# PEER expert retrieval: slots of 128 tokens and one expert each, against slots of 64 tokens and two

## The reference

```python
def blk(hb):                       # one block of 128 tokens
    q = (hb @ w_q).reshape(PEER_BLOCK, PEER_HEADS, 2, PEER_KEY_DIM // 2)
    sc = jnp.einsum('thpd,hpnd->thpn', q, sub_keys).astype(jnp.float32)
    s1, i1 = lax.top_k(sc[:, :, 0], PEER_TOPK)
    s2, i2 = lax.top_k(sc[:, :, 1], PEER_TOPK)
    cand = (s1[..., :, None] + s2[..., None, :]).reshape(PEER_BLOCK, PEER_HEADS, PEER_TOPK * PEER_TOPK)
    top_s, ci = lax.top_k(cand, PEER_TOPK)
    e = jnp.take_along_axis(i1, ci // PEER_TOPK, axis=-1) * N_KEYS \
        + jnp.take_along_axis(i2, ci % PEER_TOPK, axis=-1)
    gate = jax.nn.softmax(top_s, axis=-1).astype(hb.dtype)
    act = jax.nn.gelu(jnp.einsum('thkd,td->thk', u_tab[e], hb), approximate=False)
    return jnp.einsum('thk,thkd->td', gate * act, v_tab[e])
```

## Time and profile before

| | |
|---|---|
| median of 3 runs | 3402.43 us (3392.74 to 3404.69) |
| profiled execution | 3404.81 us, span 3403.0 us |
| PE | 2916.1 us busy, 86% |
| DVE | 2321.7 us, 68% |
| ACT | 1550.6 us, 46% |
| chain that ended last | PE 44%, DMA 27%, DVE 21% |
| moved by DMA | 1298.59 MB, mean 382 GB/s |
| of that, the gathers (queue q0) | 1140.92 MB, 82.3% of the 16 engines' time |

### The profile page before, as it was taken

How to read it: one execution, slowest core, us unless ns; L and a number is a source line. 1 busy time by engine, 2 the same in 40 slices (tenths; PEclk the granted TensorE clock), 3 DMA queues, 4 the chain that set the end, 5 groups by cost and what they waited for, 6 DMA issues and landing times.

```text
span 3403.0 us, 32496 instructions
## 1 busy us (share of the span) xinstructions
PE 2916.1 (86%) x9486; PEld 1498.2 (44%) x9486; DVE 2321.7 (68%) x5531; ACT 1550.6 (46%) x4211; POOL 1300.5 (38%) x1097
## 2 busy tenths in 40 slices
PE   7989899988889898989899878987898888787777
PEld 5755555543445444544444333533353344443222
DVE  1268738785687658774788578866876587677854
ACT  2147334554356344643456345644563455333333
POOL 0023324443344433343445434443444434343432
PEclk8998999999999999999999999999999999899899
DMA  4289999999999999999999999999999999799998
GB/s 173 90 318 362 385 384 405 392 406 418 417 392 388 422 422 408 392 399 417 421 396 414 422 421 422 405 421 422 400 373 418 422 353 330 299 373 421 372 422 346
DMA packets 238361, 1298.59 MB, mean 382 GB/s; under 512 B 45748, under 2 KB 70228, under 8 KB 95462
## 3 DMA queue, kind: packets, MB, share of 16 engines
q0 software_dynamic: 156672, 1140.92, 82.3%
q1 hardware_dynamic: 81510, 155.59, 12.2%
HBM read 1279.41 MB, written 16.44 MB: 381 GB/s over the span
## 4 chain that ended last, share of the span: by engine, by line
PE 44%; DMA 27%; DVE 21%; ACT 4%; issue 2%; POOL 0%; SPq 0%; DVEq 0%; ACTq 0%; POOLq 0%
PE PS L1080 21%; DMA R<-in_t_uv,idx 19%; DVE R L1728 8%; PE PS L763 8%; DMA R<-in_t_uv,idxS 4%; DMA wring<-in_w_out 2%; PE PS L844 2%; PE PS L1002 2%; PE PS L729 2%; PE PS L843 2%; DVE SC L1689 2%; DVE SC L1686 2%; DVE ef L1691 2%; DMA wring<-in_w_query 2%; PE PS L1029 2%
## 5 line engine op out<-in xcount | busy, mean ns | idle before, releaser
L1080 PE MATMUL PS<-R,diag 128*128 128x512 f32 x3616 | 1788.4, 630 | 295.8 <-ACT diag L1355 262.8
L694 POOL DMA_INDIRECT R<-in_t_uv,idx x1024 | 1236.6, 1208 | 1981.1 <-PE PS L1080 1236.6
L1728 DVE CUSTOM_DVE_ANT_0 R<-R,hb 128x1024 f32<-128x1024 f32 x1088 | 1316.3, 1219 | 663.0 <-DMA R<-in_t_uv,idx 581.8
L1080 PEld LDWEIGHTS PS<-R,diag 128*128 128x128 f32 x3616 | 672.1, 198 | 1172.3 <-issue 606.9
L1346 ACT ACTIVATE acts<-dots 128x1 f32<-128x1 f32 x1088 | 217.8, 200 | 1258.8 <-DVE dots L1728 1256.2
L1355 ACT ACTIVATE diag<-ident,wv 128x128 f32<-128x128 f32 x840 | 337.7, 402 | 46.3 <-PE PS L1080 19.3
L763 PE MATMUL PS<-R 128*128 128x256 f32 (+1 forms) x1280 | 296.1, 388 | 42.6 <-ACT stg L1123 36.4
L1348 ACT ACTIVATE wv<-gate,acts 128x1 f32<-128x1 f32 x1024 | 302.0, 295 | 33.2
L763 PEld LDWEIGHTS PS<-R 128*128 128x128 f32 x1280 | 245.9, 199 | 111.8 <-issue 80.2
L1739 DVE SCALAR_TENSOR_TENSOR xb<-R,wv,xb 128x1024 f32<-128x1024 f32 x184 | 235.7, 1281 | 9.5 <-ACT wv L1348 9.5
L1466 DVE CUSTOM_DVE_ANT_0 PP<-PS,mask 128x144 f32<-128x144 f32 (+7 forms) x64 | 49.4, 771 | 170.8 <-PE PS L844 170.7
(11 more groups left out here) (242 smaller groups left out, 2389.9 us busy)
## 6 DMA issues: line engine op xcount, KB each, us to landing
wring<-in_w_out SPq DMA_DIRECT2D x64, 512.0 KB, 12.0
wring<-in_w_query SPq DMA_DIRECT2D x64, 512.0 KB, 8.3
R<-in_t_win SPq DMA_DIRECT2D x27, 1024.0 KB, 12.0
R<-in_t_uv,idx POOLq DMA_INDIRECT x1024, 12.6
pr<-prd SPq DMA_DIRECT2D x8, 976.0 KB, 11.2
prd<-stg SPq DMA_DIRECT2D x54, 128.0 KB, 7.6
xb<-in_x_prompt SPq DMA_DIRECT2D x8, 512.0 KB, 8.5
R<-in_w_out SPq DMA_DIRECT2D x8, 512.0 KB, 4.7
```

The source lines that it names most:

```text
L694: e.indirect_dma_start(dst, None, table, bass.IndirectOffsetOnAxis(ap=index, axis=0)).then_inc(S[s], c.count(name, s, 16))
L1080: m = mm(bank(n), diag[:, NTH[s] % DR, :], pair(s)[:, D + 512 * n:D + 512 * n + 512], start=begins, stop=s == last_slot(t), skip_group_che ...
L1728: e.tensor_tensor_reduce(u, u, hb[:, tile_of(g) % 2, :], 1.0, 0.0, ALU.mult, ALU.add, dots[:, g % NW:g % NW + 1]).then_inc(dve_done, c.cou ...
```

## The change

A slot now holds 64 tokens and two experts of each. Partitions 0 to 63 hold the tokens with one expert, partitions 64 to 127 the same tokens with another. Slots of tokens 0 to 63 (half 0) and of tokens 64 to 127 (half 1) alternate; `place(r)` gives half and expert column of slot r: the first 8 slots of a tile are all of half 0, the last 8 of half 1, and in between they take turns. The number of slots and the bytes of each stay.

On PE `diag` becomes 128x64 (from `fold`, which has two identities of 64 on top of each other), so the product adds the two experts of each token and writes 64 partitions of PSUM, those of its half. There are 8 buffers of it. All 1024 prompt slots go to PE and none to DVE. The sample tile works as before, with two neighbouring buffers as one 128x128.

The input of a slot must stand on both halves of the partitions. So `hb` becomes `hn` (one tile's normed input) and `hh[half]`, filled by an ACT copy on the same partitions (`along`) and a DMA to the other 64 (`across`), 8 slots ahead of use. Indices and gates are written to `idxN` and `gateN`, and SP copies them to their places by four DMAs each per piece. To make room `wring` has two buffers, and `ef` shares `bposf`. The top search of the next tile begins 3 turns earlier and ends 4 turns earlier.

```diff
-DR = 4
+DR = 8
...
-def on_dve(s):
-    return s < P * NTILE and s % (4 if 4 <= s % P < 60 else 8) == 2
-
-
-BY_PE = [s for s in range(NSLOT) if not on_dve(s)]
-BY_DVE = [s for s in range(NSLOT) if on_dve(s)]
-NTH = {s: i for q in (BY_PE, BY_DVE) for i, s in enumerate(q)}
+def place(r):
+    quarter, k = divmod(r, 32)
+    if quarter in (1, 2):
+        half, n = k % 2, k // 2
+    elif k < 8:
+        half, n = 0, k
+    elif k < 24:
+        half, n = (k + 1) % 2, k // 2 - 4 + 8 * (k % 2)
+    else:
+        half, n = 1, k - 16
+    return half, 16 * quarter + n
...
-        spread(tail(t + 1), at + (52 if t > 1 else 58), at + 96)
-        spread(top(t + 1, 0), at + 96, at + 119)
+        spread(tail(t + 1), at + (52 if t > 1 else 58), at + 93)
+        spread(top(t + 1, 0), at + 93, at + 115)
...
-        wring = sb("wring", [P, 3, D])
+        wring = sb("wring", [P, 2, D])
...
-        idxS = sb("idxS", [P, NSMP], U32)
-        gateS = sb("gateS", [P, NSMP])
+        idxN = sb("idxN", [P, P], U32)
+        gateN = sb("gateN", [P, P])
...
-        hb = sb("hb", [P, 2, D])
-        diag = sb("diag", [P, DR, P])
+        hn = sb("hn", [P, D])
+        hh = sb("hh", [P, 2, D])
+        diag = sb("diag", [P, DR, 64])
...
-            return 4 if t == 1 else 3
+            return 4 if t == 1 else 2
...
-            return R[:, m % 4, :] if t == 1 else wring[:, m % 3, :]
+            return R[:, m % 4, :] if t == 1 else wring[:, m % 2, :]
...
-                if m == 2 and t > 2:
+                if m == 0 and t > 2:
...
                     yield from p.to(1 + m - nb - NCH)
                     load_w(t, m, p)
                 yield from p.to(8)
-                e.wait_ge(pe_done, c.at("pe", f"used q{t}_6"))
+                e.wait_ge(pe_done, c.at("pe", f"used q{t}_{NCH - 1}"))
                 dma(gfin, A["g_final"].partition_broadcast(P), "gfin", f"g{t}")
 
+            def norm2(p, t):
+                if t == 1:
+                    yield from p.to(3)
+                    e.wait_ge(pe_done, c.at("pe", "hT1"))
+                    across(0, 1)
+                    across(1, 1)
+
+            def across(half, t):
+                other = 1 - half
+                dma(hh[64 * other:64 * other + 64, half, :], hn[64 * half:64 * half + 64, :], f"hx{half}", f"h{t}")
+
+            def top(p, k):
+                t, piece = k // 4, k % 4
+                ne = P // pieces(t)
+                m = ne // 2
+                if t < SMP:
+                    for what, src, dst, sem in (("top", idxN, idx, "ix"), ("gate", gateN, gate, "gx")):
+                        yield from p.to(18 if what == "top" else 19)
+                        e.wait_ge(dve_done, c.at("dve", f"{what}{t}_{piece}"))
+                        for f in range(2):
+                            for half in range(2):
+                                at = 64 * half + m * piece
+                                dma(dst[64 * f:64 * f + 64, t % 2, at:at + m],
+                                    src[64 * half:64 * half + 64, ne * piece + m * f:ne * piece + m * f + m],
+                                    sem, f"{t}_{piece}" if f + half == 2 else None)
+
             def peer(g):
+                for t in range(2, NTILE + 1):
+                    if g == P * (t - 1) - 8:
+                        e.wait_ge(dve_done, c.at("dve", f"u{g - 1}"))
+                        across(0, t)
+                    if g == P * (t - 1):
+                        e.wait_ge(dve_done, c.at("dve", f"u{g - 1}"))
+                        across(1, t)
                 for t in range(1, SMP + 1):
                     if g == last_slot(t) + LAG + 3:
                         e.wait_ge(dve_done, c.at("dve", f"y{t}"))
...
-                    e.wait_ge(*spent(c, HOMES[s][1]))
+                    e.wait_ge(pe_done, c.at("pe", f"v{HOMES[s][1]}"))
...
-                    e.wait_ge(dve_done, c.at("dve", f"top{t}_{s % P * pieces(t) // P}"))
+                    e.wait_ge(S["ix"], c.at("ix", f"{t}_{s % P * pieces(t) // P}"))
...
-                    m = mm(bank(n), diag[:, NTH[s] % DR, :], pair(s)[:, D + 512 * n:D + 512 * n + 512],
-                           start=begins, stop=s == last_slot(t), skip_group_check=True)
+                    row = pair(s)[:, D + 512 * n:D + 512 * n + 512]
+                    if t == SMP:
+                        m = mm(bank(n), diagS[:, s % 4, :], row, start=begins, stop=s == last_slot(t), skip_group_check=True)
+                    else:
+                        m = mm(bank(n)[64 * half:64 * half + 64, :], diag[:, s % DR, :], row, start=s % P in (0, 8),
+                               stop=s % P in (119, 127), skip_group_check=True)
...
+            def moved(t):
+                for half in range(2):
+                    e.wait_ge(S[f"hx{half}"], c.at(f"hx{half}", f"h{t}"))
+
+            def along(half, t):
+                r = slice(64 * half, 64 * half + 64) if t < SMP else slice(0, P)
+                act(hh[r, half, :], hn[r, :], ACT.Copy).then_inc(act_done, c.count(f"hx{t}_{half}"))
+
...
-                    if h == 0 and t >= 3:
-                        e.wait_ge(dve_done, c.at("dve", f"u{last_slot(t - 2)}"))
-                    act(hb[:, t % 2, VD * h:VD * h + VD], bank(7, P, P + VD), ACT.Copy,
+                    if h == 0 and t > 1:
+                        moved(t - 1)
+                    act(hn[:, VD * h:VD * h + VD], bank(7, P, P + VD), ACT.Copy,
...
-                    act(wv[:, k:k + 1], gate_of(v), ACT.Copy, scale=acts[:, k:k + 1]).then_inc(act_done, c.count(f"w{v}"))
-                    if not on_dve(v):
-                        settle()
-                        n = NTH[v]
-                        if n >= DR:
-                            e.wait_ge(pe_done, c.at("pe", f"v{BY_PE[n - DR]}"))
-                        m = fold if tile_of(v) == SMP else ident
-                        act(diag[:, n % DR, :], m[:], ACT.Copy, scale=wv[:, k:k + 1]).then_inc(act_done, c.count(f"d{v}"))
+                    t = tile_of(v)
+                    if t < SMP and v % P % (P // pieces(t)) == 0:
+                        e.wait_ge(S["gx"], c.at("gx", f"{t}_{v % P * pieces(t) // P}"))
+                    act(wv[:, k:k + 1], gate_of(v), ACT.Copy, scale=acts[:, k:k + 1]).then_inc(act_done, c.count())
+                    settle()
+                    last = v - (4 if t == SMP else DR)
+                    if last >= 0:
+                        e.wait_ge(pe_done, c.at("pe", f"v{last}"))
+                    if t == SMP:
+                        dst, m = diagS[:, v % 4, :], fold[:]
+                    else:
+                        dst, m = diag[:, v % DR, :], fold[:, 0:64]
+                    act(dst, m, ACT.Copy, scale=wv[:, k:k + 1]).then_inc(act_done, c.count(f"d{v}"))
+                for t in range(2, SMP + 1):
+                    if g == P * (t - 1) - 8:
+                        e.wait_ge(dve_done, c.at("dve", f"u{g - 1}"))
+                        along(0, t)
+                    if g == P * (t - 1) and t < SMP:
+                        e.wait_ge(dve_done, c.at("dve", f"u{g - 1}"))
+                        along(1, t)
...
-                        act(hb[:, t % 2, :], xb[:, t % 2, :], ACT.Square, accum_out=peerv[:, 0:1]).then_inc(act_done, c.count())
+                        act(wring[:, 1, :], xb[:, t % 2, :], ACT.Square, accum_out=peerv[:, 0:1]).then_inc(act_done, c.count())
...
-                e.tensor_copy(idx[:, t % 2, cols], ef[:, hs, :].rearrange("p h k -> p (h k)")).then_inc(
+                e.tensor_copy(idxN[:, cols], ef[:, hs, :].rearrange("p h k -> p (h k)")).then_inc(
...
+                    t, half = tile_of(g), half_of(g)
+                    first = g - P * (t - 1) if g < P * NTILE + 8 else None
+                    if first == 0 or first == 8 and t < SMP:
+                        e.wait_ge(act_done, c.at("act", f"hx{t}_{half}"))
+                        if t < SMP:
+                            e.wait_ge(S[f"hx{half}"], c.at(f"hx{half}", f"h{t}"))
...
-                    e.tensor_tensor_reduce(u, u, hb[:, tile_of(g) % 2, :], 1.0, 0.0, ALU.mult, ALU.add,
+                    e.tensor_tensor_reduce(u, u, hh[:, half, :], 1.0, 0.0, ALU.mult, ALU.add,
...
-                v = g - LAG
-                if 0 <= v < NSLOT and on_dve(v):
-                    t, n = tile_of(v), NTH[v]
-                    e.wait_ge(act_done, c.at("act", f"w{v}"))
-                    if n and tile_of(BY_DVE[n - 1]) == t:
-                        e.wait_ge(dve_done, c.at("dve", f"x{BY_DVE[n - 1]}"))
-                    else:
-                        e.wait_ge(dve_done, c.at("dve", f"h{t}"))
-                    x = xb[:, t % 2, :]
-                    stt(x, pair(v)[:, D:2 * D], wv[:, v % NW:v % NW + 1], x, ALU.mult, ALU.add).then_inc(
-                        dve_done, c.count(f"x{v}"))
```

(25 more changed lines are left out.)

35 lines of the change are left out of this document (17 added, 18 removed).

## The result

| | before | changed |
|---|---|---|
| median | 3397.6 us (4 runs, 3386.7 to 3404.7) | 3523.5 us (4 runs, 3510.9 to 3526.4) |
| ratio | 1 | 1.0364, 95% interval 1.0339 to 1.0388 |
| profiled execution, span | 3404.8 us, 3403.0 us | 3522.0 us, 3520.2 us |

The changed kernel is slower by 3.6%, about 124 us. I forecast 3425 us and a range that ended at 3490.

What follows compares the result with a forecast made beforehand. The prediction took DMA's gathers, with a ceiling of 422 GB/s, to bound the kernel. Its terms -32 + 0 + 10 + 18 + 4 + 20 = +20 against 3404.8 us gave 3425 us, range 3365 to 3490.

Steps and rivals of the forecast that it cites:

- DVE's part: 184 rows of V leave DVE, 235.7 us of busy time mostly beside DMA; claimed to win 32 us.
- PE's products: PE gets 184 more V products; neighbours of opposite halves overlap in attention, waits for DMA hide the rest; cost 0.
- Rival (c): PE's column halves do not overlap, so attention's 14 extra products per tile cost +133; 3558 us, chance 0.12.
- Changes of the array's shape: Switching PE between 128-column and 64-column products, 0.1 to 0.2 us each, about three new per head; +10, bounds 0 and 29.
- New transfers: Copies of the normed input, indices and gates load the full DMA with bytes and packets; +18 us, bounds 0 and 25.
- the index's detour: SP must copy indices before POOL gathers; hidden at tile ends, exposed at the very start; +4 us (3 to 8).
- The weight ring: Matrix buffers for w_out and w_query go from three to two, so PE waits for loads; +20 us, range 0 to 112.
- rival (b): PE stands before each matrix and DMA runs dry in the tails; +60 us on top, 3465 us, chance 0.14.
- Rival (a): Relief wins: buffers come free in time and DMA is fed at 1.02 outside the sample stage; -37, 3368 us, chance 0.30.
- The DMA share in the long stretch: DMA's busy share from 600 to 2440 us, expected at 1.00 to 1.01; 1.02 near 411 GB/s would show relief winning.
- PE's waits for matrices: Sign in PE's waits for w_out and w_query loads: tens of us fit the forecast's own term, hundreds fit rival (b).
- The stretch from 2440 to 3040 us: Where the sample tile is attended; the forecast called itself wrong if this changed by more than 20 us.

## Why the prediction was wrong

The direction was right. So in the main was the bound: DMA's gathers set most of the pace, since 316 us more of work on PE cost 47. The size missed: 124 us in place of 20. By its own steps:

**DVE's part and PE's products (-32 and 0, together -32).** Measured +47 - 61 = -14. The sum is off by 18 us, and that it is no further off is luck, since the parts are not what I thought: PE's products with the relief cost 47, and it was turns that paid that back. What the relief alone is worth no run shows. Rival (c), halves that do not overlap, is dead by the rows with eight records in 1.94 us. The Trainium skill, "TensorE: Matmul & The Clock Gate", Part 3, says that matmuls in different column strips of 32 run at the same time. The trace agrees here for two halves of 64: two products take the time of one, a factor of 2.0.

**Changes of the array's shape (+10, bounds 0 and 29).** Measured +45, with what came along. "Three groups of V per head give about three new changes" is the step that failed. It was right for attention (some 200 changes) and left out the 400 to 500 of the other stages, above all the tails, where each matrix now costs two. The price of one stood in rows 5 and was right.

**New transfers (+18) and the index's detour (+4).** The copies with all seen loads ahead of them measured +28, near the sum. POOL waited for `idx` only at the very start, as forecast. The step that failed is the sentence on SP: "the waits for DVE's index stand before the weight loads of the next tile, which come 12 turns later, so nobody is late". It named only one of the things queued behind that wait. The load of `pr` stood right behind it (DVE waited 36.4 us; moving it won 15), and in tile 7 the cache loads stood between the wait and the weights (PE waited 27.4 us; moving them won 14 to 23). I had printed SP's order at a tile's end, where the first half's indices are, and not at turn 36, where the second half's are.

**The weight ring (+20, bounds 0 and 112).** The rival (b) asked for +60 more from it. (Its 3465 us is the kernel before plus 60; on top of the 20 already taken it would have been 3485.) Measured 21 in the kernel before and 36 in the changed one. Mechanism right, size within the bounds.

**Rival (a), relief wins (3368).** It did not come: even without copies and with the third buffer the kernel stays 0.9% above.

Of the signs that I named: the V products under 1871 us (that figure counts the sample tile's 256 records too; together they are 1606 + 128 = 1734), pairs within ns, DVE near 2090 (2106), the first gather 4 us later (5.0), and no rate over 422 GB/s all came. The DMA share in the long stretch was 0.99 and the rate 395 GB/s, below the 1.00 to 1.01 that I expected. PE's waits for matrices went to 154 us, between "tens" and "hundreds". The stretch from 2440 to 3040 us did change by more than 20 us: tile 7 alone took 47 more. That was the sign for "wrong", and it pointed at one of the places.

The range was too narrow since it went by the rivals, one at a time, and left no room for several terms that are off the same way. Shape (+35 over), SP's order (+29), the ring (+16), V (+18) and the copies (+6) all came out above what I took, 104 us together.

## What to carry to other kernels

When a wait is put on a queue that serves others, list everything behind it until the wait can end, at each place where it stands and not at one; here small copies of 1.05 MB in all cost 22 us themselves and some 29 more by what stood behind SP's wait for them. When a new shape of matmul comes in, count its neighbours in the whole program: here the price was paid per change, some 600 times, and it was won back only where two halves ran at once. A buffer that is free for part of a tile (the score buffer between two searches) can be worth more than the change that was planned: as a fourth weight buffer it made the kernel before 0.3% faster.

## What the hardware showed beside

Two products of 64 columns on opposite halves of the array, float32, 512 columns moving, take 1.94 us together and one takes 1.93. A wait of PE for a matrix costs more than itself: in the changed kernel's longest wait, 27.4 us in which PE stood, the granted clock falls from 0.96 to a mean of 0.57, near the lower of its two levels (1.2 of 2.4 GHz), and the matrix behind it takes 3.65 us where others take 1.98. The windows there (columns as before):

```profile
2640.00:2680.00 40.00, 31.69 (x146) 14.46 (x142) 27.60 (x45) 19.24 (x57) 19.41 (x18) 0.96 1.03 410
2680.00:2708.00 28.00, 0.57 (x2) 0.21 (x2) 8.66 (x16) 6.76 (x24) 1.77 (x2) 0.57 0.80 288
```

The same row shows what a stop of PE does to DMA: with no buffer coming free the rate falls from 410 to 288 GB/s within 28 us. The mean of a matrix's record rose from 635 and 608 ns (L1002, L1029 before) to 684 and 681. With the third buffer, and the same shapes, it is 645 to 647 and 616 to 628, so most of the rise came with the waits for the ring of two; the changes of shape are the likely rest.
